# First stage of an encoder block, tile by tile: rows normalised on VectorE alone, products begun once a tile and the first weights are split

## What is computed

```
def layer_norm(x, g, b):
    mu = jnp.mean(xf, axis=-1, keepdims=True)
    xc = xf - mu
    var = jnp.mean(jnp.square(xc), axis=-1, keepdims=True)
    y = xc * lax.rsqrt(var + LN_EPS)
    return (y * g + b)
...
    h = layer_norm(x, ln_in_g, ln_in_b)        # 512 rows of 1024
    for i in range(DEPTH):                      # DEPTH = 1
        proj = h @ w_in[i]                      # 1024 x 4608
        u, v_sg, q, k, v_sb, g_a, g_b = jnp.split(proj, IN_SPLITS, axis=-1)
```

## Time and profile before

| | |
|---|---|
| median of 3 runs | 1192.11 us (1189.66 to 1192.6) |
| the profiled execution's own time | 1189.86 us |
| its span in the profile | 1188.1 us |
| TensorE busy | 1120.9 us, 94% of the span |
| VectorE busy | 846.1 us, 71% |
| ScalarE busy | 688.6 us, 58% |
| GpSimd busy | 326.0 us, 27% |
| moved by DMA | 294.78 MB, mean 248 GB/s |

### The profile page before, as it was taken

One profiled execution on the slowest core, in us unless ns is written; L12 is line 12 of the kernel. 1 busy time (PEld: TensorE's weight loads), 2 busy tenths in 40 slices (PEclk: granted clock), 3 DMA queues, 4 the chain that ended last, 5 costly groups with the idle time before them and its releaser, 6 DMA issues.

```text
span 1188.1 us, 15715 instructions
## 1 busy us (share of the span) xinstructions
PE 1120.9 (94%) x5390; PEld 843.3 (71%) x5390; DVE 846.1 (71%) x1034; ACT 688.6 (58%) x692; POOL 326.0 (27%) x183
## 2 busy tenths in 40 slices
PE   2999999998999889999999999999999999999896
PEld 2878877777878665777777776767777777667475
DVE  7454345453444575999999988988989998887376
ACT  4431234342232432887888887777878887777344
POOL 4000000000002432444444443433444443331431
PEclk9999999998989999999999999999999999999899
DMA  7532222113234536999999999999999999998721
GB/s 284 169 105 71 71 71 70 38 36 142 73 118 175 211 111 233 348 365 373 368 375 368 368 369 355 364 357 353 363 364 358 370 371 358 363 363 266 244 110 54
DMA packets 68475, 294.78 MB, mean 248 GB/s; under 512 B 11216, under 2 KB 14288, under 8 KB 43600
## 3 DMA queue, kind: packets, MB, share of 16 engines
q1 hardware_dynamic: 52944, 256.43, 57.3%
q0 software_dynamic: 14912, 35.68, 12.2%
q10 hardware_dynamic: 576, 2.10, 0.5%
HBM read 275.29 MB, written 35.65 MB: 262 GB/s over the span
## 4 chain that ended last, share of the span: by engine, by line
PE 37%; DMA 16%; DVE 6%; ACT 3%; issue 3%; DVEq 0%; ACTq 0%; POOLq 0%; SPq 0%
DMA gu_raw<-in_moe_w_up 13%; PE ps L400 10%; PE ps L402 10%; PE ps L401 10%; PE ps L1454 3%; DVE w_lo L1653 2%; ACT w_hi L1545 2%; PE ps L1908 1%; PE ps L1194 1%; DMA gu_raw<-in_moe_w_gate 1%; DMA residual_rows<-y,put_idx 1%; DMA odd_rows<-y,put_idx 1%; PE ps L1478 1%; DVE w_lo L384 1%; PE ps L1445 1%
## 5 line engine op out<-in xcount | busy, mean ns | idle before, releaser
L1653 DVE TENSOR_TENSOR w_lo<-gu_raw,w_hi 128x2048 fp32r<-128x2048 f32 x126 | 288.5, 2290 | 52.0 <-ACT w_hi L1545 51.4
L1545 ACT ACTIVATE w_hi<-gu_raw 128x2048 fp32r<-128x2048 f32 x128 | 242.6, 1913 | 55.1 <-DMA gu_raw<-in_moe_w_up 42.9
L400 PE MATMUL ps<-w_hi,xgT_hi 128*96 128x512 f32 x512 | 205.9, 402 | 5.9 <-issue 3.2
L1756 POOL DMA_INDIRECT xg<-h_rows,get_idx x64 | 154.5, 2414 | 206.0 <-DVE get_idx L1641 156.5
L402 PE MATMUL ps<-w_hi,xgT_lo 128*96 128x512 f32 x512 | 202.9, 396 | 0.0
L401 PE MATMUL ps<-w_lo,xgT_hi 128*96 128x512 f32 x512 | 201.7, 394 | 0.0
L400 PE MATMUL ps<-w_hi,act_hi 128*128 128x512 f32 x384 | 156.4, 407 | 5.3 <-PEq L494 2.8
L401 PE MATMUL ps<-w_lo,act_hi 128*128 128x512 f32 x384 | 151.5, 394 | 0.0
L402 PE MATMUL ps<-w_hi,act_lo 128*128 128x512 f32 x384 | 151.4, 394 | 0.0
L1658 DVE TENSOR_TENSOR dn_lo<-dn_raw,dn_hi 128x2048 fp32r<-128x2048 f32 x64 | 146.0, 2282 | 4.3 <-ACT dn_hi L1551 4.1
L280 POOL TENSOR_TENSOR x_rows<-x_rows,ln_b 128x1024 f32<-128x1024 f32 x10 | 23.8, 2377 | 401.3 <-DVE x_rows L273 401.3
(11 more groups left out here) (201 smaller groups left out, 1740.6 us busy)
## 6 DMA issues: line engine op xcount, KB each, us to landing
gu_raw<-in_moe_w_gate SPq DMA_DIRECT2D x64, 1024.0 KB, 15.0
gu_raw<-in_moe_w_up SPq DMA_DIRECT2D x64, 1024.0 KB, 14.8
dn_raw<-in_moe_w_down SPq DMA_DIRECT2D x64, 1024.0 KB, 14.7
raw<-in_w_in SPq DMA_DIRECT2D x18, 1024.0 KB, 5.1
h_rows<-x_rows SPq DMA_DIRECT2D x8, 512.0 KB, 4.7
raw<-in_w_out SPq DMA_DIRECT2D x4, 1024.0 KB, 5.6
ple_raw<-in_ple_w_gate SPq DMA_DIRECT2D x4, 1024.0 KB, 10.5
x_rows<-in_x SPq DMA_DIRECT2D x4, 512.0 KB, 6.6
```

Source lines behind the costliest of these rows:

```text
L400: nc.tensor.matmul(out, x_hi, w_hi, start=first, stop=False)
L1545: nc.scalar.activation(m.w_hi[:, 2 * x.b + half], m.gu_raw[:, 2 * x.b + half], ACT.Copy).then_inc(gu_hi, 1)
L1653: nc.vector.tensor_tensor(m.w_lo[:, 2 * x.b + half], m.gu_raw[:, 2 * x.b + half], m.w_hi[:, 2 * x.b + half].bitcast(F32), ALU.subtract).th ...
L1756: nc.gpsimd.indirect_dma_start(out=m.xg[x.q][0:CAP], out_offset=None, in_=h1, in_offset=bass.IndirectOffsetOnAxis(ap=m.get_idx[x.q][0:CAP] ...
```

## The change

The loads of tiles 2 and 3 are issued behind the first two weight pieces, and the two vectors `ln_g` and `ln_b` behind tile 0. Each tile is normalised by `finish_on_vector` (already in the kernel, used for the last tile of the other two norms): (x - mean) * ln_g (L288), the reciprocal (L291), and * 1/deviation + ln_b (L297), all on VectorE. `centre` on ScalarE and `shift` on GpSimd are gone from this stage; ScalarE keeps the root and takes a root of a constant first, which loads its function table early. TensorE turns tiles 0 and 1, begins unit 0, and turns tile 2 between the halves of unit 1 and tile 3 between the halves of unit 2. Units 0 to 3 write to four banks of their own (0, 1, 2, 7) and no longer wait for a Gelu; `sg_w` is turned into bank 3. The splits of pieces 2 and 3 stand ahead of the turns of tiles 2 and 3 on ScalarE, no more behind the Gelus of units 0 and 1.

```diff
+    SGT = 3
+    FIRST_UNITS = (0, 1, 2, 7)
...
+        def unit_bank(u):
+            return FIRST_UNITS[u] if u < len(FIRST_UNITS) else MAIN[u % 2]
...
         def _(sp):
-            for t in range(NT):
+            def load_rows(t):
                 sp.dma_start(m.x[:, t], a["x"][0][t * P:(t + 1) * P, :]).then_inc(norm_semaphores.rows_in[t], 16)
-                if t == 1:
-                    norm.load_affine(sp, a["ln_in_g"], a["ln_in_b"])
+
+            load_rows(0)
+            norm.load_affine(sp, a["ln_in_g"], a["ln_in_b"])
+            load_rows(1)
             ring.load(sp, 0)
             ring.load(sp, 1)
+            load_rows(2)
+            load_rows(3)
             sp.dma_start(m.sg_w[:], a["sg_w_s"][0].rearrange("g i j -> i g j")).then_inc(small_in, 16)
+            norm.store(sp, 0, h0)
+            norm.store(sp, 1, h0)
+            ring.load(sp, 2)
+            ring.load(sp, 3)
...
-            for t in range(NT):
-                norm.store(sp, t, h0)
-            for i in range(2, DENSE_PIECES):
+            norm.store(sp, 2, h0)
+            norm.store(sp, 3, h0)
+            for i in range(4, DENSE_PIECES):
...
         def _(pool):
             set_constants(nc, m, pool, base_set, constants_set, CAP)
-            for t in range(NT):
-                norm.shift(pool, t)
...
             def unit_start(u):
 
-                if u - 2 >= 8:
+                if u < 4:
+                    return
+                if u < 6:
+                    pe.wait_ge(gelu_out, u - 3)
+                elif u - 2 >= 8:
                     pe.wait_ge(copied, u - 2 - 8 + 1)
-                elif u - 2 >= 0:
+                else:
                     pe.wait_ge(gelu_out, u - 2 + 1)
 
-            def rows_unit(u, c, t):
+            def rows_unit(u, c, t, between=None):
...
                     if half == 0 and t == NT - 1:
                         last.then_inc(half_used, 1)
+                    if half == 0 and between is not None:
+                        norm.turn(pe, between)
...
-            for t in range(NT):
-                norm.turn(pe, t)
-            for t in range(NT):
+            norm.turn(pe, 0)
+            norm.turn(pe, 1)
+            for t, between in enumerate((None, 2, 3, None)):
                 pe.wait_ge(norm_semaphores.lo_done, t + 1)
-                rows_unit(t, 0, t)
+                rows_unit(t, 0, t, between)
...
         def _(act):
-            act.wait_ge(constants_set, 1)
-            for t in range(NT):
-                norm.deviate(act, t)
-                norm.centre(act, t)
-                if t == 2:
-                    norm.high_part(act, 0)
+            act.wait_ge(base_set, 7)
+            nc.scalar.activation(m.peak[:], m.eps[:], ACT.Sqrt)
+            norm.deviate(act, 0)
+            norm.deviate(act, 1)
             ring.split_hi(act, 0)
+            norm.high_part(act, 0)
+            ring.split_hi(act, 1)
             norm.high_part(act, 1)
-            ring.split_hi(act, 1)
+            ring.split_hi(act, 2)
+            norm.deviate(act, 2)
+            ring.split_hi(act, 3)
+            norm.deviate(act, 3)
             norm.high_part(act, 2)
             norm.high_part(act, 3)
             for u in range(8):
...
-                if u < 2:
-                    ring.split_hi(act, 2 + u)
...
-            for t in range(NT):
+            def rows_statistics(t):
                 dve.wait_ge(norm_semaphores.rows_in[t], 16)
                 norm.statistics(dve, t)
-                norm.finish(dve, t)
-                if t >= 1:
-                    norm.gain(dve, t - 1)
-            norm.gain(dve, NT - 1)
-            norm.low_part(dve, 0)
-            ring.split_lo(dve, 0)
-            norm.low_part(dve, 1)
-            ring.split_lo(dve, 1)
+
+            for t in range(2):
+                rows_statistics(t)
+                norm.finish_on_vector(dve, t)
+            for t in range(2):
+                ring.split_lo(dve, t)
+                norm.low_part(dve, t)
+            rows_statistics(2)
+            norm.finish_on_vector(dve, 2)
+            rows_statistics(3)
             norm.low_part(dve, 2)
+            norm.finish_on_vector(dve, 3)
             norm.low_part(dve, 3)
             for i in range(2, 6):
                 ring.split_lo(dve, i)
```

More of the change, by code:

```diff
@@ L575, in rows_unit @@
                         kk = 4 * half + k
-                        last = product3(nc, ps[:, MAIN[u % 2]], m.act_hi[:, kk, t * P:(t + 1) * P],
+                        last = product3(nc, ps[:, unit_bank(u)], m.act_hi[:, kk, t * P:(t + 1) * P],
                                         m.act_lo[:, kk, t * P:(t + 1) * P], ring.hi(i)[:, k], ring.lo(i)[:, k],
@@ L599, in _ @@
             pe.wait_ge(constants_set, 1)
-            for t in range(NT):
-                norm.turn(pe, t)
-            for t in range(NT):
+            norm.turn(pe, 0)
+            norm.turn(pe, 1)
+            for t, between in enumerate((None, 2, 3, None)):
                 pe.wait_ge(norm_semaphores.lo_done, t + 1)
-                rows_unit(t, 0, t)
+                rows_unit(t, 0, t, between)
             pe.wait_ge(small_in, 64)
             for g in range(SGG):
-                last = nc.tensor.transpose(ps[:, YB, g * P:(g + 1) * P], m.sg_w[:, g], m.ident[:])
+                last = nc.tensor.transpose(ps[:, SGT, g * P:(g + 1) * P], m.sg_w[:, g], m.ident[:])
             last.then_inc(sg_turned, 1)
@@ L763, in _ @@
                 half = SG * (u // 4)
-                nc.scalar.activation(m.merged[:, t, half:half + SG], ps[:, MAIN[u % 2]],
+                nc.scalar.activation(m.merged[:, t, half:half + SG], ps[:, unit_bank(u)],
                                      ACT.Gelu_apprx_tanh).then_inc(gelu_out, 1)
-                if u < 2:
-                    ring.split_hi(act, 2 + u)
                 if t >= 2:
@@ L859, in _ @@
             dve.wait_ge(sg_turned, 1)
-            chained(nc.vector.tensor_copy(m.sg_wT[:], ps[:, YB].rearrange("p (g n) -> p g n", n=P)))
+            chained(nc.vector.tensor_copy(m.sg_wT[:], ps[:, SGT].rearrange("p (g n) -> p g n", n=P)))
             nc.vector.memset(m.sg_wT[HD:P, :, 0:HD], 0.0).then_inc(sg_w_ready, 1)
```

## The result

| | before | changed |
|---|---|---|
| median (range, runs) | 1191.23 us (1189.66 to 1192.6, 4) | 1177.89 us (1176.1 to 1178.36, 4) |
| ratio, 95% interval | | 0.9886, 0.9868 to 0.9903 |
| the profiled execution | 1189.86 us | 1178.36 us |
| its span | 1188.1 us | 1176.6 us |

The kernel is faster by 13.3 us. Forecast were some 7, and the measured median lies 3.1 us under the lower end of the wider range (1181.0). The forecast was laid against the profiled execution of before, 1189.86 us; between the two profiled executions the difference is 11.5 us.

What follows compares the result with a forecast made beforehand. TensorE was taken to bound the kernel: a 30.05 us start without products, then almost no gap. -10.1 + 1.8 + 1.4 = -6.9 us took 1189.86 to 1183.0, with half of 2.25 to 1184.0; range 1181.5 to 1186.5.

Steps and rivals of the forecast that it cites:

- the wider range: Whole kernel's time: the interval given 8 chances in 10, 1181.0 to 1188.5 us.
- When the first product starts: Start of the kernel: first product moves from 30.05 to 19.95 us, -10.1 us, bounds -7.8 and -10.5.
- the short price: Low part of a weight piece on VectorE: taken at 2.27 us, with 3.53 as the other end.
- The turns inside: Units 0 to 3: turns of tiles 2 and 3 now between products, 0.89 us each, +1.8 us.
- The clock at the start: First products: 12 at half rate, 7 more than before at 0.21 us, +1.4 us; ends 0 and +2.0.
- The slacks: Interleaved turns: tile 2 ready 2.0 us before TensorE needs it, tile 3 0.3 us before.
- Rival (a): Units 0 to 3: interleaving holds TensorE, gain only 4.6 us, 1186.4 us; chance 0.14.
- The sum for the first stage: Units 0 to 3 end at 45.9 us instead of 52.9: -10.1 + 1.8 + 1.4 = -6.9 us.
- Rival (c): Units 0 to 3: clock stays low through all 96 products, +12.9 us, 1203 us; chance 0.04 with its neighbours.
- Rival (b): Gain given back later, as in the experts' stage, or first product not earlier: 1190 to 1192 us; chance 0.11.
- The step that failed: Behind unit 3: all moves by the same -6.9 us, so 1189.86 becomes 1183.0, then 1184.0 us.
- half of the 2.25: Whole kernel: runs' median lay 2.25 us above the profiled execution; half was added, 1183.0 to 1184.0 us.

Runs made afterwards that it cites:

- old_norm: Changed kernel with the norm on three engines as before (`centre` on ScalarE, `shift` on GpSimd); 1187.17 us, ratio 0.9978 to the kernel before.
- old_loads: Changed kernel with the first loads in the old order (all four tiles and both vectors ahead of the weight pieces); 1181.86 us, ratio 0.9935 to the kernel before.
- again_after: The changed kernel run again, unaltered; 1180.31 us, ratio 0.9926 to the kernel before.
- after_third: The changed kernel run once more, unaltered; 1179.54 us, ratio 0.9925 to the kernel before.
- after_fourth: The changed kernel run once more, unaltered, on the same chip as filled kernels; 1180.65 us, ratio 0.9916 to the kernel before.
- warm_start: Changed kernel with 45, 28 and 20 identity transposes keeping TensorE busy until the first product; 1181.53 us, ratio 0.9937 to the kernel before.
- shift_16: Changed kernel with 16 more transposes ahead of the turn of `sg_w`; 1182.38 us, ratio 0.9944 to the kernel before.
- the four filled ones: 18 transposes in each of two standstills, two runs per kernel: kernel before 1185.53 and 1186.46 us, changed kernel 1179.67 and 1177.77 us.
- combined: Changed kernel with transposes at the start and in both stops, and ScalarE's small operations ahead of long ones; 1174.53 us, ratio 0.9873 to the kernel before.

## Why the prediction was wrong, step by step

**When the first product starts:** -10.1 forecast, -10.76 in the recorded trace (30.05 to 19.29) and -10.63 between the second traces of both kernels (29.37 to 18.74). `ln_b` 1.6 us earlier, not 1.0; the splits at the short price, 2.28. old_norm shows the long one beside GpSimd's add, and there 4.01 us: the step had the right cause, and its upper end of 3.53 was too low. old_loads puts the order of the loads at 2.1 us.

**The turns inside:** +1.8 forecast. A turn and the three products behind it take 1.58 us (30.13 to 31.71), less 3 x 0.23 is 0.89, as forecast.

**The clock at the start:** 12 products at half rate forecast, where before has four and a part of one more (the prediction counts it as five). The recorded trace has 12 and a part of one more (19.29 to 24.87), again_after nearly 13, after_third 11 and a part, but after_fourth seven (from 18.95), by its timeline:

```profile
21.25 0.63 PE L402 MATMUL ps<-w_hi,act_lo 128*128 128x512 f32 x1
21.67 0.57 PE L400 MATMUL ps<-w_hi,act_hi 128*128 128x512 f32 x1
22.08 0.39 PE L401 MATMUL ps<-w_lo,act_hi 128*128 128x512 f32 x1
```

The page "TensorE: Matmul & The Clock Gate" of the Trainium skill (Part 1, on the warm-up) says that the number varies from run to run, and these traces agree: 7, 11, 12 and 13. It hardly moves the end of the stage (45.07 with seven against 45.16 with 13), because with fewer the slack at the turn of tile 2 is used up: after_fourth waits 0.31 us there, and warm_start, with none, 1.21.

**The slacks:** 2.0 us at the turn of tile 2 forecast, 1.2 found (ready at 28.91, turned at 30.13); 0.3 at that of tile 3, 0.35 found (36.18, 36.53). Rival (a) did not come true here (no wait in the recorded trace, 0.31 us in after_fourth), but old_norm is its case: a norm that is late inside costs a wait at each turn and the clock.

**The sum for the first stage:** -6.9 forecast, -7.25 measured, and -7.2 to -7.5 among the repetitions. This much of the prediction was right. Rival (c), a fallen clock for all 96 products, is refuted. Rival (b), that the gain is lost in the experts' stage, did not come true either: its first product starts 10.4 us earlier and its last 11.2.

**The step that failed** is the one from that sum to the time: "this gives 1183.0 [...] so I add half of it: 1184.0". It holds that everything behind unit 3 moves by the same amount ("Whatever moves the first product also moves what follows"), and its range had no term for what could differ there. I had the row of it in hand, the standstill of 2.79 us with 14 products at half rate behind it, and used it only as a price for the start. Both traces of before have this stretch, 3.0 us. Of the four of the changed kernel the recorded one and after_third lack it, after_fourth has 8 of the 14 products and again_after all. So the recorded pair differs by 7.25 us up to this stop and by 10.1 behind it, and over all these traces the difference that the stops add is 2.2 us in the mean; with the stops filled it is 0.6. The term that I put at nothing thus measured 2.2 us in the mean and 3 in the pair that was recorded.

Of the some 9 us that the repetitions show, 7.3 are the first stage, which stands in every trace, and the clock behind the stops accounts for the rest within what the intervals allow. The other 4 us or so of the recorded 13.3 did not come again. The experts' stage, whose length differs by 4 us between executions of one kernel, makes 0.8 of the 11.5 us between the recorded traces. That the first executions were a draw to both sides (before 2.0 us above its later mean, the changed kernel 2.7 below) is argued, not shown. Even the repeated changed kernel, at 1179.5 to 1180.7, lies under the range by 0.3 to 1.5 us, partly because I added half of the 2.25: before has medians of 1188.35 to 1190.19 over 15 to 19 executions on each of four chips, so the profiled 1189.86 was no low value.

**What stays open:** whether the fall of the clock at the first stop is rarer in the changed kernel by its nature or by chance (over all kernels, 14 half-rate products in four of four traces whose first stage ends after 51 us and in two of eight others speak for its nature, but those are few, and no row shows how the one would set the other), and what sets the length of the experts' stage in one execution.

## What to carry to other kernels

When a step early in a program is sped up and the engine that bounds it has no gap afterwards, the gain passes through, but each later standstill of TensorE may cost a different amount in the next execution (here 0 to 3 us behind a stop of 2.8): price each one seen in the trace, and widen the range by them. Start the products when one tile and one piece are ready and put late tiles between products; here a norm inside that order did better on one engine, with its little operations ahead of the long ones on the others. Before sizing an effect under half a per cent, look at how single executions scatter and not at three of them.

## What the hardware showed that I had not expected

- After a stop of 2.79 to 2.82 us, with the same instructions before and after it, 14 products ran at half rate, or six to eight (in shift_16 after two at full rate), or none; one kernel showed 14, 8 and none in four executions. Behind a stop of 3.08 to 3.09 us it was 7 to 13 in twelve of twelve traces. The two levels of the clock are 1.2 and 2.4 GHz (0.43 and 0.23 us from one product to the next).
- Transposes of the identity, which do no work for the result, in both stops kept the clock at full rate behind them in five of five traces (the four filled ones and combined), with 0.82 to 0.86 us of idle time left in the first stop and 1.12 to 1.15 in the second. Such transposes also bring the clock up: in warm_start TensorE ran nothing else before the turn at 11.62, and that took 1.16 us for eight, not 1.94.
- Ahead of the first product the windows of the changed kernel (10 to 20 us) read a granted clock of 1.00 while the turns took 1.94 us for eight; the rate is to be read from the distances of the instructions there.
- A subtraction of 128 x 2048 values on VectorE took 2.28 us alone, 3.53 where 1.38 us of it lay beside a GpSimd addition, and 4.01 where it was 1.87 (old_norm): 1.25 and 1.73 longer, nearly the whole overlap. That they exclude each other was known to the prediction, the sizes were not.
